# First attention: q's halves stacked on the partitions, a column of ones in v, moves begun by SyncE

## The reference, cut to what matters

```python
q = rms_norm(q.reshape(b, n, 16, 64), q_norm)      # k alike, 4 heads; both rotated for latent tokens
s = jnp.einsum('bqhgd,bkhd->bhgqk', qi, k, preferred_element_type=jnp.float32) * dk ** -0.5
p = jax.nn.softmax(s, axis=-1).astype(v.dtype)
o = jnp.einsum('bhgqk,bkhe->bqhge', p, v)
```

## Time and profile before

| | us |
|---|---|
| median of 3 runs (lowest, highest) | 2858.99 (2853.84, 2862.96) |
| the profiled execution | 2859.39 |
| its span in the trace | 2857.6 |
| PE, DVE, ACT, POOL busy | 2601.8, 1448.4, 1042.1, 734.2 |
| mean granted clock of TensorE | 0.965 of full |

### The profile page before, as it was taken

One profiled execution on the slowest core, in us unless ns is written; L12 is line 12 of the kernel. 1 busy time (PEld: TensorE's weight loads), 2 busy tenths in 40 slices (PEclk: granted clock), 3 DMA queues, 4 the chain that ended last, 5 costly groups with the idle time before them and its releaser, 6 DMA issues.

```text
span 2857.6 us, 39059 instructions
## 1 busy us (share of the span) xinstructions
PE 2601.8 (91%) x16373; PEld 1446.0 (51%) x16584; DVE 1448.4 (51%) x2179; ACT 1042.1 (36%) x1713; POOL 734.2 (26%) x985
## 2 busy tenths in 40 slices
PE   4889999799999998799999999886988998899997
PEld 1456665555556576367554445544543333344443
DVE  2447883854332215789664422655765643433322
ACT  2436772423321114667443322322342223422221
POOL 0210000347778703300040000033343543011100
PEclk7998999999999999999999999998989999999998
DMA  6220004255552211210145532221112323233331
GB/s 223 104 89 16 2 2 151 101 183 180 185 182 82 94 63 47 75 48 2 45 133 177 180 101 90 93 89 52 45 53 73 105 73 103 59 103 104 100 98 54
DMA packets 206079, 268.26 MB, mean 94 GB/s; under 512 B 8976, under 2 KB 188559, under 8 KB 196687
## 3 DMA queue, kind: packets, MB, share of 16 engines
q1 hardware_dynamic: 199758, 243.97, 26.6%
q0 software_dynamic: 5280, 18.64, 1.9%
q10 hardware_dynamic: 864, 3.15, 0.3%
HBM read 252.62 MB, written 10.49 MB: 92 GB/s over the span
## 4 chain that ended last, share of the span: by engine, by line
PE 71%; DVE 15%; ACT 5%; issue 3%; POOL 3%; DMA 2%; SPq 0%; POOLq 0%; DVEq 0%; ACTq 0%
PE PS L289 20%; PE PS L288 20%; PE PS L290 19%; PE PS L863 2%; PE PS L490 2%; DVE WB L284 2%; DVE SM L945 2%; DVE AR L951 2%; ACT WB L274 1%; DMA WS<-in_mlp_w 1%; DVE X L1228 1%; DVE GT L1237 1%; DMA WS<-in_w_ada 1%; PE PS L2011 1%; PE PS L881 1%
## 5 line engine op out<-in xcount | busy, mean ns | idle before, releaser
L289 PE MATMUL PS<-H,WB 128*128 128x512 bf16 (+1 forms) x1953 | 686.9, 352 | 30.6 <-DVE WB L284 10.5
L288 PE MATMUL PS<-H,WB 128*128 128x512 bf16 (+2 forms) x1907 | 669.3, 351 | 28.7 <-DVE WB L284 14.7
L290 PE MATMUL PS<-H,WB 128*128 128x512 bf16 (+2 forms) x1949 | 684.2, 351 | 1.2
L284 DVE TENSOR_TENSOR WB<-WS,WB 128x2048 bf16<-128x2048 f32 (+3 forms) x165 | 376.3, 2282 | 571.4 <-ACT WB L274 571.3
L274 ACT ACTIVATE WB<-WS 128x2048 bf16<-128x2048 f32 (+3 forms) x165 | 295.5, 1792 | 652.5 <-PE PS L290 424.9
L288 PE MATMUL PS<-AR,WB 128*128 128x512 bf16 (+1 forms) x1279 | 431.6, 337 | 15.8 <-DVE WB L284 7.7
L289 PE MATMUL PS<-AR,WB 128*128 128x512 bf16 (+1 forms) x1280 | 431.7, 337 | 8.1 <-DVE AR L1627 4.8
L290 PE MATMUL PS<-AR,WB 128*128 128x512 bf16 (+1 forms) x1281 | 431.7, 337 | 1.1
L288 PEld LDWEIGHTS PS<-H,WB 128*128 128x128 bf16 x1976 | 195.1, 99 | 295.3 <-issue 59.7
L290 PEld LDWEIGHTS PS<-H,WB 128*128 128x128 bf16 x1976 | 195.6, 99 | 176.2 <-issue 7.9
L289 PEld LDWEIGHTS PS<-H,WB 128*128 128x128 bf16 x1976 | 195.5, 99 | 166.4 <-issue 7.6
(11 more groups left out here) (399 smaller groups left out, 3766.8 us busy)
## 6 DMA issues: line engine op xcount, KB each, us to landing
WS<-in_mlp_w SPq DMA_DIRECT2D x64, 1024.0 KB, 5.5
WS<-in_w_ada SPq DMA_DIRECT2D x48, 1024.0 KB, 5.0
WS<-in_w_in SPq DMA_DIRECT2D x26, 1024.0 KB, 5.1
WS<-in_ada_w SPq DMA_DIRECT2D x24, 1024.0 KB, 5.0
WS<-in_ffn_w_in SPq DMA_DIRECT2D x44, 512.0 KB, 4.8
e_scratch<-EB POOLq DMA_DIRECT2D x16, 512.0 KB, 3.7
EB<-e_scratch POOLq DMA_DIRECT2D x16, 512.0 KB, 3.7
WS<-in_ffn_w_out SPq DMA_DIRECT2D x8, 1024.0 KB, 5.2
```

Of the source, the lines that this page charges most:

```text
L284: e.tensor_tensor(lo, staged(i), hi, SUB).then_inc(dv.sem, dv.mark(("lo", i)))
L288: e.matmul(out_, l[0], r[0], start=start, stop=False)
L289: e.matmul(out_, l[0], r[1], start=False, stop=False)
L290: return e.matmul(out_, l[1], r[0], start=False, stop=stop)
```

## The change

The high and low halves of a q unit are now written to the unit's own `sq` buffer. SP begins four transfers for each q unit that bring them to `q_` so that a head's high half lies on 64 partitions and its low half on the other 64. The scores are then two matmuls with contraction over 128 partitions, (high + low) by high of k and (high + low) by low of k, where there were three over 64 (the product low by low, which was left out before, is now in the sum). Each head of v has a 65th column, ones in the high half and zeros in the low, so that the weighing gives the row sums; exp of the first attention no longer accumulates, and the reciprocal reads PSUM. The output transposes, `out_high` and `out_low` come one step later (i-6), in the second attention too. ScalarE waits, before it squares unit u, for the moves of unit u-6.

```diff
+        def q_halves(u):
+            raw, sq, n = qkv_bufs(u)
+            return sq.bitcast(BF)[:, 0:n], sq.bitcast(BF)[:, n:2 * n]
...
+        def q_moves_sp(e):
+            for i, last in ((1, ("ada0", 11)), (2, ("ada0", 13)), (3, ("ada0", 15)), (4, ("wo0", 0, 0))):
+                load_tiles(e, tile_of.get(last, 0) + 1)
+                for u in range(4 * i - 3 if i > 1 else 0, min(4 * i + 1, 16)):
+                    key, s = QU[u]
+                    hi, lo = q_halves(u)
+                    q = at_q[u % 6]
+                    po.wait_ge(e, ("q low", u))
+                    e.dma_start(q_at(2 * key, LO, s), hi[LO]).then_inc(q.sem, q.mark())
+                    e.dma_start(q_at(2 * key, HI, s), lo[LO]).then_inc(q.sem, q.mark())
+                    e.dma_start(q_at(2 * key + 1, HI, s), hi[HI]).then_inc(q.sem, q.mark())
+                    e.dma_start(q_at(2 * key + 1, LO, s), lo[HI]).then_inc(q.sem, q.mark(("q", u)))
...
                 pe.wait_ge(e, ("qkv", key, s))
-                if u > 5:
+                if u > 5 and QU[u - 6][0] < 8:
+                    at_q[u % 6].wait_ge(e, ("q", u - 6))
+                elif u > 5:
                     dv.wait_ge(e, ("turned", u - 6))
                 e.activation(sq, ps(bank_of["qkv", key, s], n), SQUARE)
...
+            e.memset(VH[0][:, :, :, 64:65], 1.0).then_inc(po.sem, po.mark())
+            e.memset(VH[1][:, :, :, 64:65], 0.0).then_inc(po.sem, po.mark("v ones"))
...
-                    m = mm3(e, at(("S", t, u), c1 - c0, c0), q, [x[:, k0 + c0:k0 + c1] for x in k], True, True)
+                    if A.stacked:
+                        e.matmul(o, q, x[0], start=True, stop=False)
+                        m = e.matmul(o, q, x[1], start=False, stop=True)
+                    else:
+                        m = mm3(e, o, q, x, True, True)
...
-                if whole := Q.group_at(i - 5):
+                if whole := Q.group_at(i - 6):
                     out_turn(*whole)
...
+                if A.stacked:
+                    e.activation(Q.p(u), Q.scores_at(u), EXP, bias=Q.largest(u))
+                    return
...
+                if A.stacked:
+                    pe.wait_ge(e, ("O", A.tag, g))
+                    e.reciprocal(sums, A.O_at(g)[:, :, 64]).then_inc(dv.sem, dv.mark())
```

More of the change, by code:

```diff
@@ L148, in build @@
         at_s5c = [done(f"s5c{i}_landed", 16) for i in range(2)]
+        at_q = [done(f"q{i}_landed", 16) for i in range(6)]
         at_kpe, at_qpe = done("kpe_landed", 16), [done(f"qpe{i}_landed", 16) for i in range(4)]
@@ L608, in build @@
         k_ = arena2(6144, 4, TOK)
-        V_ = arena2(12288, 6, 256)
+        V_ = arena2(12288, 6, 260)
+        VH = [V_[:, i, :, :].rearrange("p a (h n) -> p a h n", n=65) for i in range(2)]
         QT = [arena(17664 + i * 512, 512) for i in range(12)]
@@ L727, in first @@
                     old = QU[u - 6][0]
-                    (po if old < 8 else dv).wait_ge(e, ("q" if old < 8 else "k", u - 6))
+                    (po if old < 8 else dv).wait_ge(e, ("q low" if old < 8 else "k", u - 6))
                 ac.wait_ge(e, ("sq", u))
@@ L933, in divide @@
                 ac.wait_ge(e, ("exp", t, u))
-                e.reciprocal(sums, sums).then_inc(dv.sem, dv.mark())
-                pe.wait_ge(e, ("O", A.tag, g))
+                if A.stacked:
+                    pe.wait_ge(e, ("O", A.tag, g))
+                    e.reciprocal(sums, A.O_at(g)[:, :, 64]).then_inc(dv.sem, dv.mark())
+                else:
+                    e.reciprocal(sums, sums).then_inc(dv.sem, dv.mark())
+                    pe.wait_ge(e, ("O", A.tag, g))
                 if g > 1:
@@ L938, in divide @@
                 dv.wait_ge(e)
-                e.tensor_tensor(A.OT[g % 2].rearrange("p (h n) -> p h n", n=64), at(("O", A.tag, g), 256).rearrange("p (h n) -> p h n", n=64), sums.unsqueeze(2).to_broadcast([128, 4, 64]), MUL).then_inc(dv.sem, dv.mark(("out", A.tag, g), ("free", ("O", A.tag, g))))
+                e.tensor_tensor(A.OT[g % 2].rearrange("p (h n) -> p h n", n=64), A.O_at(g)[:, :, 0:64], sums.unsqueeze(2).to_broadcast([128, 4, 64]), MUL).then_inc(dv.sem, dv.mark(("out", A.tag, g), ("free", ("O", A.tag, g))))
             def largest(u):
@@ L966, in attention_dve @@
                     low(i - 2)
-                if whole := Q.group_at(i - 5):
+                if whole := Q.group_at(i - 6):
                     out_low(*whole)
-        GP = [arena(13824 + i * 768, 768) for i in range(3)]
+        GP = [arena(13848 + i * 768, 768) for i in range(3)]
         GPT = [arena2(9216 + i * 768, 6, 128) for i in range(3)]
-        GOT = [arena(16128 + i * 256, 256) for i in range(4)]
+        GOT = [arena(16152 + i * 256, 256) for i in range(4)]
         def gqa_q(e, h, j):
             u = QU.index((h // 2, 0 if j < 4 else 1))
-            po.wait_ge(e, ("q", u))
-            r = HI if h % 2 else LO
-            return [q_[r, i, h // 2, j * 128:(j + 1) * 128] for i in range(2)]
+            at_q[u % 6].wait_ge(e, ("q", u))
+            return q_[:, h % 2, h // 2, j * 128:(j + 1) * 128]
         def gqa_k(e, h):
@@ L984, in gqa_k @@
             dv.wait_ge(e, ("k", QU.index((i, 0))), ("k", QU.index((i, 1))))
-            r = HI if h % 2 else LO
-            return [k_[r, 0, h // 4, :], k_[r, 1, h // 4, :]]
+            return [k_[:, i, h // 4, :] for i in range(2)]
         def gqa_v(base):
```

35 lines of the change are left out of this document (21 added, 14 removed).

## The result

The changed kernel takes 2829.53 us (median of 4 runs, 2826.64 to 2830.89); the kernel before takes 2857.86 (4 runs, 2853.84 to 2862.96). The ratio is 0.990, with a 95% interval of 0.9888 to 0.9913. That is 28.3 us less; the forecast was 15 less, and the time lies 1.5 us under the range's lower end. The profiled execution took 2828.37 us with a span of 2826.5, against 2859.39 and 2857.6 before.

A forecast was written before the change was run, and what follows sets the result against it. TensorE was taken to set the first attention's pace, VectorE not far behind. The terms, -17 - 1.5 - 1.5 + 0.2 + 2.2 + 2.0 = -15.6 us, took 2859.4 to 2843.8, given as 2844, range 2831 to 2854.

The forecast's parts named there:

- The triple: First attention, spacing of context maxima: from 6.40 to 5.87 us (VectorE floor 5.39, waits 0.48 including 0.06 late scores), saving 17.
- rival B: First attention: VectorE runs nearly without waits, 5.5 us a triple, saving 28, so 2833; chance 0.12.
- rival A: First attention: ScalarE's and the output's waits stay whole, saving 11 instead of 17, so 2850; chance 0.15.
- The question becomes which of VectorE's waits remain: First attention: TensorE, at 4.45 of 6.40 us a triple, no longer the bound; VectorE's remaining waits decide, 0.48 a triple.
- the six changes: First attention, TensorE: switches between 64- and 128-row matmuls, 0.10 to 0.15 us each, some 0.8 a triple, all go.
- TensorE at 75 to 80%: Sign to look for in the first attention: TensorE's busy share falls to near 75 to 80%.
- The slow stretch: 17 us at the 1.2 GHz clock in the first attention may shorten: 1.5 us saved, bounds 0 and 4.
- The moves: QKV stage: ScalarE's wait at unit 6 costs 2.2 us, the slow clock after TensorE's pause 2.0 (0 to 3.5).
- Rival D: QKV stage: moves hold up the weights, three QKV tiles each some 5 us late, +13, so 2857; chance 0.08.
- Second attention: Output transposes a step later wait less for low halves: 1.5 us saved, between 1 lost and 4.9 saved.
- C: Rival, first attention: TensorE's clock falls to 1.2 GHz repeatedly, 8.9 us a slow triple, up to 2889; chance 0.05.
- E: Rival, first attention: something unseen keeps the pace at 6.40, only small terms left, 2859 to 2863; chance 0.03.

The follow-up runs named there:

- experiment 1: Changed kernel with a third matmul of 128 rows in every score (k's low-half product added twice): 2835.33 us, ratio 0.9917, triple 5.98.
- 8: Changed kernel with the row maximum of each context unit taken twice, more work for VectorE: 2831.13 us, ratio 0.9903, triple 5.73.
- experiment 9: Changed kernel with TensorE's transposes issued ahead of the scores in the first attention: 2902.37 us, ratio 1.0161, triple 7.88.
- 5: The kernel before, unchanged, profiled once more (also written "before again"): 2851.26 us in a single execution, triple 6.40.
- experiment 2: The kernel before with two matmuls of 64 rows per score in the first attention instead of three, no moves: 2840.74 us, ratio 0.9934, triple 5.95.
- experiment 12: The kernel before with only the output transposes and their halves one step later (i-6), both attentions: 2856.38 us, ratio 0.9992, triple 6.32.
- after again: The changed kernel, unchanged, profiled once more: 2830.27 us in a single execution, triple 5.68.
- 3: Changed kernel with the output transposes and their halves back at i-5, both attentions: 2833.51 us, ratio 0.9911, triple 5.74.
- 4: Changed kernel without the column of ones in the weighing; exp accumulates row sums again, reciprocal moved back: 2833.91 us, ratio 0.9911, triple 5.78.
- Experiment 7: Changed kernel with the moves of units 0 and 1 begun earlier, after ada0 9: 2826.32 us, ratio 0.9882, QKV 128.0.
- experiment 10: Changed kernel with each move cut into two of 32 rows, 128 transfers: 2840.9 us, ratio 0.9947, QKV 148.9.

## Why the prediction went as it did

The forecast was 15.6 less; the medians differ by 28.3, the two profiled executions by 31.0. The first attention gave 26.2 where its terms came to 18.3. Of these 7.9 some 6 are in the triple and 2 in the slow stretch. The rest of the miss is in no term that a run shows, as the sum below says.

**The triple, the step that failed.** The forecast was 5.39 + 0.48 = 5.87, and 5.68 was measured. The mis-sized term is the floor of VectorE, 5.39. It was made of busy time plus the small gaps in a stretch with many stops, 5.28 + 0.10. Measured are 5.11 busy and 0.41 waiting for ScalarE, and 0.16 of other gaps fills it up to 5.68. Without its waits for ScalarE the triple is 5.68 - 0.41 = 5.27 long, where the forecast put 5.39. The busy part fell by 0.17, most of it because instructions in a dense stretch overlap by some 0.08, the rest because they are a few ns shorter. The 0.06 for late scores is gone as well. Over 30.1 triples the 0.19 is 5.7 us; 30.1 x 5.68 = 171 instead of 177, so 23.0 saved and not 17. It lay inside the step's own bounds (11 to 32), nearer to rival B's 5.5 a triple than to rival A. The step also called this floor the pace of the kernel, and that held only in part, as the next paragraph says.

**"The question becomes which of VectorE's waits remain".** Half right. The waits for ScalarE came in the sum as forecast, but VectorE is not the bound by itself: 0.33 more work for it cost 0.05, and 0.76 more for TensorE, which the forecast had freed, cost 0.29. What fits all of experiments 1, 8 and 9 is a ring: three engines hand on work through two banks, and its round trip sets the pace. That is argued from these three and from the chain, not shown by taking the ring away: a third bank for the transposes would test it, and wasn't tried. It would also say why the third matmul (0.76) and the six changes (0.8) did not give 1.56 a triple: TensorE was spared them, and the triple gave back 0.72. By the corners, and subtracting 0.06 for the turn and 0.10 for the ones (as if these added), the 128 rows gave 6.40 - (5.98 + 0.16) = 0.26 with three matmuls and 5.95 - (5.68 + 0.16) = 0.11 with two. The third matmul gave the most, 0.29 to 0.45.

The Trainium skill, TensorEngine Tiling (Array Packing), Key Properties, says that a change of tiling mode drains the engine. The traces fit it where TensorE nearly sets the pace: ten of thirty groups of six transposes at 0.66 in experiment 1, none under 0.80 before. What the rule does not give is the time of a kernel that TensorE does not bound.

**TensorE at 75 to 80%.** Wrong: 111.79 of 120 is 93%. Its rows seem to count the wait for the bank as busy: six transposes show as 0.83 to 1.01 in its chain, and the 0.76 that experiment 1 adds to a triple raised the busy time by only 0.5. The share can't be read as load.

**The slow stretch.** Forecast 1.5, between 0 and 4. Take attention less 32 triples, which holds the slow clock and also the start and the end of the stage: 10.2 us before (215.0 - 204.8), 6.9 after (188.8 - 181.9), so 3.3. That is near the upper bound of 4. Over all kernels of the next sentences the same difference is 11.0 and 6.4, so 4.6, which is above it. In all four kernels with 64-row scores (before, 5, 2, 12) the clock fell to 1.2 GHz within 5 us of the first row maximum. In the nine with 128 rows and the change's order of scores and transposes it did not fall in the first 10 us. But in experiment 9, also with 128 rows, it fell 3.6 us after the first row maximum. And in the four TensorE's pause for the first exp was longer, 1.71 to 2.14 us, against 1.10 to 1.52 in the nine. So the rows and the length of that pause are not told apart, and the cause stays open.

**The moves.** The wait at unit 6 was forecast at 2.2, and 2.55 was measured; the slow clock behind it at 2.0. Mean QKV of the seven kernels with moves as in the change (after, after again, 1, 3, 4, 8, 9) is 134.0, of the four without (before, 5, 2, 12) 129.9: 4.1 against the 4.2 forecast. Single profiles differ by 3 to 4 us within each set, so a match as close as that is luck in part. Experiment 7 takes it all away. Rival D did not happen, but experiment 10 shows that it is one doubling away.

**Second attention.** Nothing of the 1.5 is to be seen in the wait: the output transposes waited 4.9 us in 15 places, and in the changed kernel (1211 to 1371 us) just as much:

```profile
PE PS L919 <- DVE AR L996: 4.9, 15, 0.3
```

The stage's length differs by 2.0 between the two first profiles (151.6 and 149.6), but the kernels spread over as much: 148.7 to 151.6 in all, with means of 151.0 for the four that turn at i - 5 and 150.1 for the ten that turn at i - 6. The step that failed here is that VectorE makes up part of the division within one step.

**The other rivals.** A gave 2850 and is out: the waits are 0.41 a triple and not 0.70. C is out: the clock is 1.00 in 240 to 400 us. The prediction's sign of being wrong, a dip of the granted clock inside the attention, did come, but only for some 3 us within 229 to 237. The rule on which it leaned, the Trainium skill's "A second HAM failure mode: psum-queue depth-cycling" on TensorE: Matmul & The Clock Gate, did not show itself; even experiment 9, with TensorE busy 80.44 of 120 us, ran at 1.00. E is out. B was the nearest in time, 2833, and wrong in its reason: VectorE's waits stayed.

**The sum.** -23.0 for the triples, -3.3 for the stretch, +4.1 for the moves: -22.2. The 0.2 for the reciprocal at the end of the stage was not measured apart. The medians differ by 28.3, with 24.9 to 32.0 by the interval. In the two first profiled executions, 31.0 apart, the stages are -26.2 for the attention, +1.5 for QKV (132.2 against 130.7), -2.0 for the second attention and -2.2 for what comes before the first rotation multiply, which is at 87.5 and at 85.3 us, and in all kernels between 83.1 and 87.5 (83.6 for before again, so this is no effect of the change). That leaves 2.1. So of the whole gain some 6 us of the difference of the medians, beyond the terms, have no owner that an experiment shows.

## What to carry to other kernels

Busy time plus gaps overstates the floor of an engine that stops often; take the spacing of starts in a stretch where it does not stop. When the bound engine is relieved, look for a ring through buffers before naming the next engine: add work to each suspect in turn and see what the pace gives. Small transfers issued from the weights' queue cost SyncE by count (the same for 32 rows and 64), so place the first of them by what reuses their source.

## What the runs showed of the hardware that was not expected

- A pause alone does not decide TensorE's clock. The same pause of 3.65 us in the QKV stage, at the same instruction, came with a fall to a mean of 0.57 in the kernel before, and with none in the changed kernel, where the clock is at 1.00 from 176 to 190 us:

```profile
180.67 0.66 PE L506 MATMUL PS<-KM,STAT 128*128 128x128 f32 x4 [3.65 <-ACT STAT L500]
```

```profile
176.00:190.00 14.00, 10.35 (x59) 6.13 (x58) 5.69 (x8) 6.07 (x10) 3.09 (x3) 1.00 0.60 183
```

- 16 to 17 us at 1.2 GHz at the start of the attention repeat in both profiles of the kernel before; the other two with 64-row scores have some 7 and 10 us (experiment 2) and 10 and 3 (experiment 12) there. With 128 rows none or at most some 7 us come. The one spot of the changed kernel, from 233 us, follows a pause of TensorE of 2.47 us, behind VectorE's half of a weight cast; in experiment 1 a pause of 2.15 us at the same place came with no fall:

```profile
231.86 0.44 PE L901 MATMUL PS<-KM,AR 128*128 128x128 f32 x2 [2.47 <-DVE AR L996]
```

- A transfer inside SBUF takes SyncE 0.59 to 0.60 us to issue in the median, with 32 rows or 64. A 1 MB weight tile took 0.38 before, and 0.59 right behind the moves.
- Reading v's heads of 65 columns from odd columns costs nothing that shows, 0.03 us a matmul.
